# Expert layers whose matmuls walk the tokens in another order

## What is computed

```python
u = peer_u[ec]                                   # ec: the 128 experts of a token
act = jax.nn.gelu(jnp.einsum('tkd,td->tk', u, xc))
return jnp.einsum('tk,tkd->td', gc * act, peer_v[ec])
```

## Time and profile before

| | |
|---|---|
| median of 3 runs | 3883.01 us (3880.59 to 3890.09) |
| the profiled execution's own time | 3889.79 us |
| its span, first to last instruction | 3888.0 us |
| mean granted TensorE clock | 0.981 |
| TensorE matmuls busy | 3715.0 us, 96% |
| GpSimd, VectorE, ScalarE busy | 2462.6, 2048.7, 1565.6 us |
| peer_u0, peer_u1 | about 2256 to 2642 us, 3008 to 3390 us |

### The profile page before, as it was taken

The page is one execution under the profiler, slowest core; times in us unless marked ns, Lnnn a source line. Parts: engine busy times, 40 slices in busy tenths (PEclk is TensorE's granted clock), DMA queues, the critical chain, the costliest instruction groups (busy, mean ns, idle before and its releaser), DMA issues.

```text
span 3888.0 us, 72695 instructions
## 1 busy us (share of the span) xinstructions
PE 3715.0 (96%) x30508; PEld 3595.5 (92%) x30508; DVE 2048.7 (53%) x2953; ACT 1565.6 (40%) x1974; POOL 2462.6 (63%) x970
## 2 busy tenths in 40 slices
PE   6999998999999989999999999999999999999998
PEld 3799897899998888999999999999999999999998
DVE  6676256773434454454113589584444666544445
ACT  5413433333333334454444433434444343444443
POOL 0147983797795756779888879207888100188876
PEclk9999999999999999999999999999999999999999
DMA  8467652564553433545555545445555444455543
GB/s 328 177 239 266 267 214 87 195 240 162 207 213 114 155 129 120 187 151 184 181 187 187 183 173 182 174 166 181 184 187 191 165 179 176 173 184 185 187 163 124
DMA packets 98269, 714.38 MB, mean 184 GB/s; under 512 B 11024, under 2 KB 11152, under 8 KB 12048
## 3 DMA queue, kind: packets, MB, share of 16 engines
q1 hardware_dynamic: 97056, 703.65, 49.4%
q10 hardware_dynamic: 1008, 7.79, 0.5%
HBM read 709.30 MB, written 2.10 MB: 183 GB/s over the span
## 4 chain that ended last, share of the span: by engine, by line
PE 75%; POOL 11%; DVE 7%; issue 4%; ACT 2%; DMA 1%; DVEq 0%; POOLq 0%; SPq 0%; ACTq 0%
PE bank L504 48%; PE bank L1006 19%; POOL unit_lo L462 11%; PE bank L633 2%; DMA ring<-in_w 1%; DVE unit_lo L1698 1%; PE bank L533 1%; PE bank L572 1%; PE bank L957 1%; ACT unit_hi L1053 1%; PE bank L516 0%; PE bank L742 0%; PE bank L909 0%; DVE ada_acc L1522 0%; DVE c_raw L2065 0%
## 5 line engine op out<-in xcount | busy, mean ns | idle before, releaser
L462 POOL TENSOR_TENSOR unit_lo<-ring,unit_hi 128x1024 fp32r<-128x1024 f32 x956 | 2437.6, 2566 | 1315.3 <-ACT unit_hi L1053 1313.4
L1053 ACT ACTIVATE unit_hi<-ring 128x1024 fp32r<-128x1024 f32 x1204 | 1239.2, 1055 | 1233.9 <-PE bank L504 537.5
L504 PE MATMUL bank<-xl_hi,unit_hi 128*128 128x256 f32 x4976 | 1414.5, 284 | 48.8 <-POOL unit_lo L462 28.0
L504 PE MATMUL bank<-xl_lo,unit_hi 128*128 128x256 f32 x4976 | 1397.7, 281 | 0.0
L504 PE MATMUL bank<-xl_hi,unit_lo 128*128 128x256 f32 x4976 | 1397.3, 281 | 0.0
L504 PEld LDWEIGHTS bank<-xl_hi,unit_hi 128*128 128x128 f32 x4976 | 943.1, 190 | 60.4 <-POOL unit_lo L462 24.9
L504 PEld LDWEIGHTS bank<-xl_hi,unit_lo 128*128 128x128 f32 x4976 | 943.3, 190 | 0.0
L504 PEld LDWEIGHTS bank<-xl_lo,unit_hi 128*128 128x128 f32 x4976 | 942.6, 189 | 0.5
L1006 PE MATMUL bank<-w_r,unit_hi 128*128 128x256 f32 x4096 | 723.9, 279 | 4.0 <-DVE w_r L2467 4.0
L1006 PEld LDWEIGHTS bank<-w_r,unit_hi 128*128 128x128 f32 x4096 | 625.4, 187 | 4.3 <-issue 4.3
L1006 PE MATMUL bank<-w_r,unit_lo 128*128 128x256 f32 x2048 | 572.4, 279 | 0.0
(11 more groups left out here) (421 smaller groups left out, 4869.5 us busy)
## 6 DMA issues: line engine op xcount, KB each, us to landing
ring<-in_w SPq DMA_DIRECT2D x669, 1024.0 KB, 4.8
resid<-in_xT ACTq DMA_DIRECT2D x1, 2048.0 KB, 15.7
tmp_ctx<-in_ctxT ACTq DMA_DIRECT2D x1, 2048.0 KB, 11.5
rnn_gates<-in_rgw ACTq DMA_DIRECT2D x1, 2048.0 KB, 9.5
out<-resid SPq DMA_DIRECT2D x4, 512.0 KB, 2.6
con<-in_con ACTq DMA_DIRECT2D x1, 512.0 KB, 3.3
con<-in_con ACTq DMA_DIRECT2D x1, 448.0 KB, 7.9
p_tmp<-in_pT ACTq DMA_DIRECT2D x1, 256.0 KB, 3.3
```

Of the source, the lines that this page charges most:

```text
L462: pool.tensor_tensor(lb[b][:], ring[slot][:, f * HALF:(f + 1) * HALF], hb[b][:].bitcast(F32), ALU.subtract).then_inc(lo_done, 1)
L504: mm = pe.matmul(bank[(s.t0 + tile[m]) % TILES][:, 0:T], w[b][:, (i % 8) * P:(i % 8 + 1) * P], mv[x][:, k, :], start=(k == 0 and w is hb a ...
L1053: act.activation(hb[b][:], ring[slot][:, f * HALF:(f + 1) * HALF], ACT.Copy).then_inc(hi_done, 1)
```

## The change

In peer_u0 and peer_u1 a matmul no longer walks its 256 tokens from 0 to 255 in units j = 1, 2, 3 of each four. The row is cut into `blocks` equal parts, and the walk takes `run_` tokens of the first part, `run_` of the second and so on, then the next `run_` of each. With (2, 8) it goes 0..7, 128..135, 8..15, 136..143. The moving operand and the output take the same order, so each token's result lands in its place. Unit j = 0 keeps (1, T), the plain order.

| unit | peer_u0: blocks, run | peer_u1: blocks, run |
|---|---|---|
| j = 0 | 1, 256 | 1, 256 |
| j = 1 | 2, 8 | 2, 4 |
| j = 2 | 8, 4 | 2, 16 |
| j = 3 | 2, 32 | 4, 4 |

```diff
--- before.py
+++ after.py
@@ -55,6 +55,9 @@
 NG = KC // GR
 BIG = 3.0e38
 GATE_UP = 2.0 ** 15
+
+
+TURNS = {"peer_u0": [(1, T), (2, 8), (8, 4), (2, 32)], "peer_u1": [(1, T), (2, 4), (2, 16), (4, 4)]}
 SCALE = 192.0 ** -0.5
 
 
@@ -486,6 +489,12 @@
 
                 n_tiles = s.tiles // len(movs)
                 n = s.n0 + j + it * s.npi
+                blocks, run_ = TURNS[s.name][j % 4] if s.name in TURNS else (1, T)
+
+                def in_turn(ap):
+                    if blocks == 1:
+                        return ap
+                    return ap.rearrange("p (h q c) -> p q h c", h=blocks, c=run_)
                 for f in range(2):
                     b = (2 * (s.n0 + j) + f) % NBUF
                     pe.wait_ge(lo_done, 2 * n + f + 1)
@@ -501,8 +510,8 @@
                             pe.wait_ge(tile_free[s.eng], s.base + tile[-1] + 1 + it * (s.npi * s.tiles))
                         for w, x in ((hb, 0), (hb, 1), (lb, 0)):
                             for m, mv in enumerate(movs):
-                                mm = pe.matmul(bank[(s.t0 + tile[m]) % TILES][:, 0:T],
-                                               w[b][:, (i % 8) * P:(i % 8 + 1) * P], mv[x][:, k, :],
+                                mm = pe.matmul(in_turn(bank[(s.t0 + tile[m]) % TILES][:, 0:T]),
+                                               w[b][:, (i % 8) * P:(i % 8 + 1) * P], in_turn(mv[x][:, k, :]),
                                                start=(k == 0 and w is hb and x == 0),
                                                stop=(k == per_tile - 1 and w is lb))
                     mm.then_inc(half_done, 1)
```

## The result

The changed kernel took 3924.37 us (median of 4 runs, 3921.69 to 3926.61) against 3886.11 us of the kernel before in 4 runs, a ratio of 1.0091 with a 95% interval of 1.0071 to 1.0111. I had forecast no change with 0.54 and slower with 0.38. The time lies inside the range given, but the likeliest case was the wrong one.

What follows compares the result with a forecast made beforehand. TensorE's matmul pace was taken to bound the changed stages. With 0 us added for jumps, the profiled execution's 3889.8 us stayed 3889.8 us and the median 3883 us, the forecast; range 3868 to 3985 us.

Steps and rivals of the forecast that it cites:

- the likeliest case: Whole kernel: no measurable change, within 0.3%, chance 0.54, own range 3874 to 3894 us.
- What bounds the kernel: peer_u0 and peer_u1: TensorE is busy nearly throughout, so the price of a changed matmul (117.8 ns before) counts in full.
- The jumps' number: Changed matmuls of peer_u0 and peer_u1: 190,464 runs in all; 0.061 ns per run reaches the 0.3% bound (11.6 us).
- What I take: Changed matmuls: price of a jump set at 0 ns, between nothing or a small gain and +452 us.
- the rows nearest in kind: Profile rows of the kernel before, for TensorE's moving operand and VectorE's PSUM reads, read as showing jumps for nothing.
- The pool product: TensorE matmul L719, plain fp32, reading four runs of 64: 215.9 ns a record against 216.0 without jumps, so jumps cost nothing.
- VectorE's rows: L2420 and L2434: PSUM reads with jumps and in sequence both take 1.04 ns an element, so jumps are free.
- rival A: TensorE's walk over SBUF or PSUM: each jump costs array steps, +80 us at one step (0.42 ns) a run; chance 0.31.
- the clean step: TensorE's column time at 2.4 GHz, 0.417 ns, against 0.452 ns a column for the matmuls before the change.
- Rival B: Changed matmuls' output: jumps break up pairs or lines, the walk falls to about half its rate, +452 us; chance 0.07.
- Rival C: Changed matmuls: other orders are quicker by avoiding memory conflicts, at most 9.8 ns each, -45 us; chance 0.08.
- The control inside the trace: The unit of each four that keeps its plain order in peer_u0 and peer_u1: it must stay at 117.8 ns a matmul.

Runs made afterwards that it cites:

- fp32 experiment: Changed kernel with units 1 (4 blocks in runs of 4) and 3 (plain order) of each four in peer_u0 multiplied as plain fp32: 4404.25 us.
- bf16 units: Units 1 to 3 of each four, against the changed kernel, multiply constants viewed as bf16, in partly other orders: 3871.16 us in one run.
- reading-only run: Changed kernel with only the moving operand walked in turn and the output written in plain order: 3921.12 us, ratio 1.0077.
- steps of 4 and 8: Against the changed kernel, weight loads take 128 words with steps of 2, 4 or 8 words, under partly other orders: 4267.94 us in one run.

## Why the prediction was wrong

**What bounds the kernel: right.** TensorE's pace per matmul counted in full. The paces sum to 32.2 us and the stages grew by 33 us. Nothing hid it and no new wait came.

**The jumps' number: right, but not the measure.** 32.2 us over 190,464 runs make 0.17 ns a run, nearly three times the 0.061 ns at which I said it decides. Yet the price is not one per run: 0.10 to 0.28 ns in the changed kernel, and less than nothing in four other orders.

**The step that failed** is "What I take. I take 0 ns", by the rows nearest in kind. The pool product could not show the price, on two counts: it is fp32, and its runs are 64 words long, which cost nothing in fp32r either (2 in 64: 117.7 ns). I had written that a jump could hide in the slower walk and show in the faster one, and chose the row all the same. The fp32 experiment shows it: 215.7 ns a record with 64 runs where fp32r lost 17.7 ns. VectorE's rows spoke of another engine's read, and of PSUM, which was never the place. The sum should have gone by the sentence in rival A: the matmuls' pace was already 8% off the clean step, so something on that path had no slack. The bf16 units (109.1 ns) show that it goes with the 4 bytes a number, and the reading-only run that the order's price arises in the moving operand's read.

**Rival A (0.31)** is what happened in direction and place. Its price of one array step a run (+80 us) was 2.5 times too high, and its signature, a pace that rises with the runs, holds only roughly: 8 in 4 has twice the runs of 2 in 8 and 0.9 ns more, and 4 in 4 twice the excess of 2 in 4 with as many runs.

**Rival B (0.07)** did not occur: writing in turn left every unit at 5.74 us.

**Rival C (0.08)** had a true core. The change's six orders were all slower or level, but 8 in 8 gains 2.6 of the 9.8 ns that I gave as the most. My argument against it, that the excess looks like a fixed rate, does not hold: with whole pieces of 16 bytes the orders give anything from 115.2 to 140.9 ns, and the plain order itself has a second pace of 113.3 ns.

**The control inside the trace** worked as said: 5.73 us for the plain units beside the changed ones (but for the one at 113.3 ns), so nothing beside the order made the loss.

**What stays open:** which part of the memory two addresses must share for the read to wait. The distances tried (16 to 128 words) order the paces by no rule that I found. Whether weight load and moving operand meet there was not settled: steps of 4 and 8 made the load the longer of the two, and step 2 (121.7 and 120.0 ns) can be read both ways. What sets a plain stretch at 117.8 or at 113.3 ns is open too, and this rival, that the timing of load and matmul to each other counts and not only the addresses, stands untested. That 16 bytes is the piece in which the operand is fetched is worked out from some of the paces (runs of 2, step 4), and 2 in 2 speaks against the simple form of it.

## What to carry to other kernels

A row that shows a thing for nothing speaks only for its own rate. Before using it for another data type, look whether the path has slack there: a dense fp32r matmul of 256 columns takes 117.8 ns where bf16 takes 109, and there the order in which the moving operand is read changed the time, while the dearest order was free in fp32, and runs of 8 were free in bf16. Compare the runs' lengths too. In fp32r keep runs of at least 4 words; the output's order in PSUM was free with such runs. Where TensorE's fp32r pace sets the end, try orders: 8 blocks in runs of 8 gave 1.3% of the whole kernel for one `rearrange` around the operands of two matmul lines. And judge an order by units that alternate with plain ones in one trace, for a plain stretch moves by 4% on its own.

## What the runs showed of the hardware that I had not expected

- A read order can be quicker than the plain one beside it: 115.2 ns (8 in 8), 115.4 ns (4 in 4 at 80 words) against 117.8 ns.
- The same plain fp32r matmuls run at 117.8 ns in most dense stretches and at 113.3 ns in some, for hundreds or thousands in a row, at the same granted clock.
- Runs of 2 words (8 bytes) in fp32r take 173.2 to 226.8 ns, up to about twice the plain order. The Trainium skill (Advanced Engine Details and Errata, Memory Cachelines) gives SBUF lines of 16 bytes and says that two hits on a line absorb the access time. Lines of 16 bytes fit most of these paces, though not that of 2 in 2 (173.2 ns); the two hits do not fit, as every run of 2 hits its line twice and the matmuls still take 1.5 to 1.9 times as long.
- 4 blocks in runs of 4 go from 135.5 to 115.4 ns when the blocks lie 80 in place of 64 words apart.
- A weight load with a step of 4 words takes 233 ns for 128 words and then sets the matmuls' pace.
